# Earlier transfers in the even layer: load stage, attention projection, cached pages and sample outputs

## Chip, cores and metric

The kernel runs on one core of a Trainium2 chip. The metric is device time in microseconds for one execution. The engines of the core are TensorE (PE; its weight loads are shown as PEld), VectorE (DVE), ScalarE (ACT), GpSimd (POOL) and SyncE (SP). SP computes nothing here and issues nearly all transfers; its queue is shown as SPq.

## The reference

One inference step of a two-layer decoder trunk on a prompt of 1024 tokens and eight samples of four new tokens with a paged cache of 256 tokens each. Width 1024, all in float32. What matters here is the start of the first (even) layer:

```python
mod = silu(c) @ w_mod[l] + b_mod[l]
shift, scale, gate = split(mod, 3)
h = rms_norm(x, norm_w[l]) * (1 + scale) + shift
q_a, g_a, kv_a, z_a, z_b, xbc, dt_raw = split(h @ w_in_even)
q, k_cmp, k_slc, k_win = rope(...)              # rotary positions
past_kv = cache_nsa[page_table]                 # 8 samples x 2 pages of 128 tokens
kc, vc = compress(k_cmp), compress(v_cmp)       # silu((block + pe) @ w1) @ w2, blocks of 32 tokens
o = g0 * attend(q, kc, vc) + g1 * attend(q, ks, vs) + g2 * attend_window(q, kw, vw)
o_a = o * silu(z_a)
```

The prompt and the samples use the same weights. Later come a state-space mixer and the output projection of this layer, then a gated linear attention layer; the change doesn't touch them.

## The kernel before

The program is a sequence of blocks. In each one, every engine has its own list of instructions, the lists are tied by semaphores, and the block ends with a barrier of all engines. Work of one block therefore can't overlap that of the next, except for transfers that an earlier block issued and didn't wait for.

`block_load` (L212 to L363) brings in the rows of x, normalises them and transposes them into `hT`. It forms the modulation of layer 0 in two kinds, shift (i = 0) and scale (i = 1): `mod_products` on TensorE (64 matmuls for each half of 512 columns, banks 6 and 7), a copy on ScalarE, `mod_turn`, then `mod_finish` on VectorE. Last, ScalarE and VectorE apply scale and shift to `hT`. SP issues in this order: constants, c, x, four halves of w_mod of 2 MB each with one semaphore for each kind, the mask table, and the two attention weight tiles `w_attn[0]` and `w_attn[1]`, for which only the next block waits.

`block_attn_proj` (L379 on) projects to q (chunk 0), gates and the first part of kv (chunk 1) and the rest of kv (chunk 2), each in `NT` = 9 groups (one of samples, eight of 128 prompt rows). `w_attn` has two slots; slot 0 is loaded again for chunk 2. SP loads the rotation table and `pe_rows` at the head of the block, and TensorE's first instruction waits for both (`rope_in`). After chunk 2 SP writes the new kv rows out and waits for these writes at the end.

`block_past` (L609 on) reads the 16 cached pages into four slots of `page_rows`, each with one transfer from the page pool and one from the window cache. TensorE transposes each page, and behind every second page it does one of eight z products with the weights `w_za`. SP issues, after page 3, the eight transfers of `w_za`, and after page 5 the compression weights (four transfers of 0.5 MB) and `cmp_w2`. Page i waits until page i - 4 is transposed. Then TensorE runs the compression.

`block_attn_samples` (L741 on) attends for the samples. It writes its result to the scratch tensor `o_save` in memory, waits, reads it back as rows into `A.o_smp`, and waits again.

`block_attn_prompt` (L895 on) attends for the prompt in 72 units: for each of eight row tiles one compressed unit and eight others. For each unit TensorE does scores, transposes of the probabilities (`turn`) and values. The transposes are in groups, numbered in order; the number's parity gives the PSUM bank (4 or 5) and the engine that copies the group out (even: VectorE, odd: ScalarE). Group 0 was the turn of the sample outputs, ahead of all units. Behind the units 6, 14, 22 and so on stands a job of the late modulation.

## Time and profile before

| | us |
|---|---|
| median of three runs | 1896.12 |
| range of the runs | 1893.22 to 1897.64 |
| the profiled execution | 1895.02 |
| its span, first to last instruction | 1893.2 |

| stage (profiled execution) | begins at |
|---|---|
| block_load | 0 |
| block_attn_proj | 54.40 |
| block_past | 230.29 |
| block_attn_samples | 328.08 |
| block_attn_prompt | 378.42 |

TensorE is busy for 1667.0 us, 88% of the span; VectorE 39%, ScalarE 31%, GpSimd 20%. The mean granted clock of TensorE is 0.938 of full speed. The profile's page shows the whole; the views used below are the waits (who stood idle, and what released it), the timeline (instructions in order of time, with the idle time before them in brackets), the windows (busy time of each engine, granted clock and share of the DMA engines in a stretch) and the transfers with the time from issue to landing.

### The profile page before, as it was taken

The page shows a single profiled execution, that of the slowest core. Times are in us where ns is not written, and L with a number is a line of the kernel's source. Part 1 is how long each engine was busy: PE and PEld are TensorE (multiplying, and loading weights), DVE is VectorE, ACT ScalarE, POOL GpSimd, SP SyncE. Part 2 cuts the span into 40 slices and gives each one's busy share as a digit, 9 for nine tenths or more (in the row PEclk, how much of TensorE's full clock was granted, in tenths as well). Part 3 has the DMA queues.
Part 4 walks back from the last instruction along what each step waited for, and adds up shares of the span by engine and source line. Part 5 has one row for each costly group of instructions (what it writes and reads, how often), then busy time and mean ns, then how long its engine had stood idle before and what let it go on. Part 6 is the DMA issues. An engine that isn't in the chain of part 4 may idle for free. (4 is left out here: it accounts for less than half of the span.)

```text
span 1893.2 us, 27343 instructions
## 1 busy us (share of the span) xinstructions
PE 1667.0 (88%) x11621; PEld 1275.7 (67%) x11621; DVE 746.1 (39%) x1231; ACT 584.0 (31%) x1098; POOL 378.7 (20%) x234
## 2 busy tenths in 40 slices
PE   4799678699989879999999958898899989998698
PEld 4345447466666659999988736784899965554475
DVE  2211110145555546661078834223321444444443
ACT  4001110155544443222145533323330402222221
POOL 1111000011000012332179734110221230000231
PEclk8899889799999989999989978998899989998699
DMA  9120282142211001111101155112100130002521
GB/s 336 45 77 1 74 200 61 40 136 71 87 46 46 1 6 36 50 49 35 37 23 34 41 144 174 49 46 71 47 23 14 43 100 1 23 23 84 219 89 61
DMA packets 120573, 129.93 MB, mean 69 GB/s; under 512 B 16726, under 2 KB 92936, under 8 KB 120324
## 3 DMA queue, kind: packets, MB, share of 16 engines
q1 hardware_dynamic: 120100, 128.08, 21.6%
q8 instruction: 92, 1.51, 0.3%
q0 software_dynamic: 352, 0.10, 0.2%
q14 instruction: 29, 0.24, 0.0%
HBM read 107.05 MB, written 23.18 MB: 69 GB/s over the span
## 5 line engine op out<-in xcount | busy, mean ns | idle before, releaser
L154 PE MATMUL banks<-h_T_rest,w_ssd_high 128*128 128x352 f32 x480 | 156.0, 325 | 0.0
L154 PE MATMUL banks<-h_T_high,w_ssd_high 128*128 128x352 f32 x480 | 155.8, 325 | 0.0
L154 PE MATMUL banks<-h_T_high,w_ssd_rest 128*128 128x352 f32 x480 | 155.2, 323 | 0.0
L154 PE MATMUL banks<-w_attn,h_T 128*128 128x408 f32 (+5 forms) x432 | 147.8, 545 | 0.0
L154 PEld LDWEIGHTS banks<-w_attn,h_T 128*128 128x128 f32 (+1 forms) x432 | 73.9, 183 | 72.8 <-issue 55.6
L1165 DVE TENSOR_REDUCE neg_max_att<-banks 128x1 f32<-128x640 f32 (+7 forms) x128 | 88.8, 702 | 83.6 <-PE banks L154 83.3
L154 PE MATMUL banks<-w_r,h_T 128*128 128x512 f32 (+1 forms) x320 | 118.1, 556 | 0.0
L154 PE MATMUL banks<-out_even_w_high,mix_high 128*128 128x512 f32 (+1 forms) x216 | 87.9, 407 | 16.2 <-DVE out_even_w_rest L2070 12.3
L1104 ACT ACTIVATE p_att<-banks,neg_max_att 128x640 f32<-128x640 f32 (+7 forms) x128 | 89.6, 703 | 24.4 <-DVE neg_max_att L1165 23.7
L1042 PE MATMUL banks<-const_f,p_att 128*128 128x128 f32 x544 | 83.3, 285 | 15.1 <-DVE p_T_att L1170 8.3
L154 PEld LDWEIGHTS banks<-h_T_high,w_ssd_rest 128*128 128x128 f32 x480 | 90.9, 189 | 0.0
L154 PEld LDWEIGHTS banks<-h_T_high,w_ssd_high 128*128 128x128 f32 x480 | 90.2, 188 | 0.6 <-issue 0.6
L154 PEld LDWEIGHTS banks<-h_T_rest,w_ssd_high 128*128 128x128 f32 x480 | 90.1, 188 | 0.0
L1042 PEld LDWEIGHTS banks<-const_f,p_att 128*128 128x128 f32 x544 | 57.6, 141 | 47.7 <-issue 14.0
L154 PE MATMUL banks<-w_v_high,h_T_high 128*128 128x256 f32 (+1 forms) x288 | 82.9, 288 | 6.7 <-POOL w_v_rest L2398 6.7
L154 PEld LDWEIGHTS banks<-w_r,h_T 128*128 128x128 f32 (+1 forms) x320 | 50.2, 176 | 56.6 <-issue 55.1
L154 PE MATMUL banks<-out_even_w_rest,mix_high 128*128 128x512 f32 (+1 forms) x216 | 86.9, 402 | 0.0
L154 PE MATMUL banks<-out_even_w_high,mix_rest 128*128 128x512 f32 (+1 forms) x216 | 86.7, 401 | 0.0
L2751 DVE SCALAR_TENSOR_TENSOR gla_state<-gla_state,chunk_decay,banks 128x256 f32<-128x256 f32 x128 | 52.2, 475 | 86.4 <-PE banks L154 86.4
L1376 POOL TENSOR_TENSOR w_ssd_rest<-w_ssd,w_ssd_high 128x1024 fp32r<-128x1024 f32 x20 | 58.5, 2925 | 124.3 <-ACT w_ssd_high L1329 124.3
L154 PE MATMUL banks<-w_v_rest,h_T_high 128*128 128x256 f32 (+1 forms) x288 | 82.4, 286 | 0.0
L154 PE MATMUL banks<-w_v_high,h_T_rest 128*128 128x256 f32 (+1 forms) x288 | 81.7, 284 | 0.0
(475 smaller groups left out, 3496.6 us busy)
## 6 DMA issues: line engine op xcount, KB each, us to landing
w_mod_late<-in_w_mod_dram SPq DMA_DIRECT2D x8, 2048.0 KB
w_ssd<-in_w_in_even_dram SPq DMA_DIRECT2D x20, 512.0 KB, 3.8
w_mod_rows<-in_w_mod_dram SPq DMA_DIRECT2D x4, 2048.0 KB, 20.9
xin<-in_x_prompt_dram SPq DMA_DIRECT2D x8, 512.0 KB, 6.1
page_rows<-in_cache_nsa_dram SPq DMA_DIRECT2D x16, 256.0 KB, 2.7
cmp_w<-in_nsa_cmp_w_dram SPq DMA_DIRECT2D x8, 512.0 KB
silu_z_T<-in_state_ssd_dram SPq DMA_DIRECT2D x8, 512.0 KB, 4.3
out_dram<-silu_z_T SPq DMA_DIRECT2D x8, 512.0 KB, 3.5
```

The lines of the kernel that those rows point to most:

```text
L154: return nc.tensor.matmul(out, lhsT, rhs, start=start, stop=stop, skip_group_check=True)
L1042: last = nc.tensor.transpose(e.ps[:, 4 + g % 2, x * P:(x + 1) * P], src, e.ident)
L1104: nc.scalar.activation(p[:, n % 2, g, 0:counts[n] * P], head_scores(n, g), ACT.Exp, bias=neg[:, n % 4, g:g + 1], accum_out=den[:, i % 2, b ...
L1165: nc.vector.tensor_reduce(neg[:, n % 4, g:g + 1], head_scores(n, g), AX.X, ALU.max, negate=True).then_inc(neg_ready, 1)
L1376: nc.gpsimd.tensor_tensor(wlo[:, f % 2, :, :], w[:, f % 2, :, :], whi[:, f % 2, :, :].bitcast(F32), ALU.subtract).then_inc(w_rest, 1)
L2751: nc.vector.scalar_tensor_tensor(S[:, (n + 1) % NS, h, :], S[:, n % NS, h, :], Q.eb[:, h, n:n + 1], e.ps[:, j, x * LV:(x + 1) * LV], ALU.m ...
```

## The change

In the load stage each half of the modulation weights has a semaphore of its own, and TensorE waits for each half ahead of its products. The rotation table and the `pe_rows` are issued between the two attention weights. VectorE's copy of the masks moves behind the first `mod_finish`.

In the attention projection SP loads the page table and two pages at the head, and the `z_a` weights after chunk 1, into the place of slot 1 of `w_attn`. The pages lie where `o_smp`, `vcd` and `vcs` lie later, so GpSimd's memset of `vcd` now waits for the last page's transposes. `block_past` begins with page 2.

The sample outputs are read back by the first two transfers of the prompt attention, and they are turned and multiplied behind unit 8, as a group between those of the units. The groups of units 0 to 7 have numbers lower by one, so bank and copying engine are swapped for them; from unit 9 on they are as before.

```diff
@@ block_load
-        wmod_in = [new_sem(nc, f"w_mod_in{i}") for i in range(2)]
+        wmod_in = [[new_sem(nc, f"w_mod_in{i}{half}") for half in range(2)] for i in range(2)]
...
                 sp.dma_start(masks[:, :], e.k_masks).then_inc(masks_in, 16)
-                for i in range(2):
-                    load_attn_w(sp, e, e.w_attn[:, i], e.w_attn_in[i], ATTN_COLS[i])
+                load_attn_w(sp, e, e.w_attn[:, 0], e.w_attn_in[0], ATTN_COLS[0])
+                sp.dma_start(e.rope[:, :, :, :], e.k_rope.rearrange("p (a m d) -> p a m d", a=2, m=NT)).then_inc(e.rope_in, 16)
+                for j in range(2):
+                    sp.dma_start(e.pe_rows[:, j, :], e.nsa_cmp_pe[0].rearrange("v c d -> (v c) d")).then_inc(e.rope_in, 16)
+                load_attn_w(sp, e, e.w_attn[:, 1], e.w_attn_in[1], ATTN_COLS[1])
...
                 for i in range(2):
-                    pe.wait_ge(wmod_in[i], 32)
                     if i:
                         pe.wait_ge(mod_rows, i)
-                    mod_products(nc, e, wm[:, i, :, 0:512], 6)
-                    mod_products(nc, e, wm[:, i, :, 512:1024], 7).then_inc(mod_done, 1)
+                    for half in range(2):
+                        pe.wait_ge(wmod_in[i][half], 16)
+                        last = mod_products(nc, e, wm[:, i, :, half * 512:(half + 1) * 512], 6 + half)
+                    last.then_inc(mod_done, 1)
...
-                dve.wait_ge(masks_in, 16)
-                nc.vector.tensor_copy(e.kb[:, :], masks[:, :])
                 for i in range(2):
                     dve.wait_ge(mod_turned, i + 1)
                     mod_finish(nc, e, link, 0, i, 4, 0)
                     dve.sem_inc(mod_taken, 1)
+                    if i == 0:
+                        dve.wait_ge(masks_in, 16)
+                        nc.vector.tensor_copy(e.kb[:, :], masks[:, :])
@@ helpers
+PAGES_EARLY = 2
+
+def page_slot(A, i):
+
+    return A.pages[i % 4 // 2][:, i % 2, :]
+
+def load_page(sp, e, A, numbers, i):
+
+    number = sp.value_load(numbers[0:1, i:i + 1], min_val=0, max_val=NPOOL - 1)
+    src = e.cache_nsa[0][bass.ds(number, 1), :, :, :, :].rearrange("n t a g d -> (n t) (a g d)")
+    sp.dma_start(page_slot(A, i)[:, 0:512], src).then_inc(A.page_in[i % 4], 16)
+    sp.dma_start(page_slot(A, i)[:, 512:768], e.cache_nsa_win[0, i // NPG, (i % NPG) * PAGE:(i % NPG + 1) * PAGE].rearrange("t a g d -> t (a g d)")).then_inc(A.page_in[i % 4], 16)
@@ block_attn_proj
             def _(sp):
-                sp.dma_start(rope[:, :, :, :], e.k_rope.rearrange("p (a m d) -> p a m d", a=2, m=NT)).then_inc(rope_in, 16)
-                sp.dma_start(per[:, 0, :], e.nsa_cmp_pe[0].rearrange("v c d -> (v c) d")).then_inc(rope_in, 16)
-                sp.dma_start(per[:, 1, :], e.nsa_cmp_pe[0].rearrange("v c d -> (v c) d")).then_inc(rope_in, 16)
+                sp.dma_start(numbers[:, :], e.page_table.rearrange("b n -> (b n)").rearrange("(a n) -> a n", a=1)).then_inc(pt_in, 16)
+                sp.wait_ge(pt_in, 16)
+                for i in range(PAGES_EARLY):
+                    load_page(sp, e, A, numbers, i)
                 sp.wait_ge(proj_done, NT)
                 load_attn_w(sp, e, w[:, 0], w_in[0], cols[2])
...
+                sp.wait_ge(proj_done, 2 * NT)
+                wv = e.w_in_even[0, :, E_ZA:E_ZB].rearrange("(k p) n -> p k n", p=P)
+                for hh in range(HG):
+                    for g in range(G):
+                        sp.dma_start(A.w_za[:, :, hh * P + g * HD:hh * P + (g + 1) * HD], wv[:, :, (g * HG + hh) * HD:(g * HG + hh + 1) * HD]).then_inc(A.w_za_in, 16)
                 sp.wait_ge(rot_done, 3 * NT)
@@ block_past
-                for i in range(NP):
+                for i in range(PAGES_EARLY, NP):
                     if i >= 4:
                         sp.wait_ge(tr_done, i - 3)
...
-                    if i == 3:
-                        wv = e.w_in_even[0, :, E_ZA:E_ZB].rearrange("(k p) n -> p k n", p=P)
-                        for hh in range(HG):
-                            for g in range(G):
-                                sp.dma_start(A.w_za[:, :, hh * P + g * HD:hh * P + (g + 1) * HD], wv[:, :, (g * HG + hh) * HD:(g * HG + hh + 1) * HD]).then_inc(w_za_in, 16)
+                    load_page(sp, e, A, pt, i)
...
             def _(pool):
+                pool.wait_ge(tr_done, NP)
                 nc.gpsimd.memset(A.vcd[:, :, :], 0.0).then_inc(zeroed, 1)
@@ block_attn_samples
                 sp.wait_ge(o_out, 16 * DB)
-                for g in range(G):
-                    dst = A.o_smp[:, :].rearrange("p (h g d) -> p h g d", h=HG, g=G)[:, :, g, :]
-                    sp.dma_start(dst, e.o_save[:, g * HG * HD:(g + 1) * HG * HD].rearrange("t (h d) -> t h d", d=HD)).then_inc(o_out, 16)
-                sp.wait_ge(o_out, 16 * (DB + G))
@@ block_attn_prompt
+SAMPLES_AT = 8
...
-    engine_of.append(0)
-    order_of.append(1)
-    totals[0] = 1
...
+        if n == SAMPLES_AT:
+            sample_group = len(engine_of)
+            engine_of.append(0)
+            totals[0] += 1
+            order_of.append(totals[0])
...
             def _(sp):
+                for g in range(G):
+                    dst = A.o_smp[:, :].rearrange("p (h g d) -> p h g d", h=HG, g=G)[:, :, g, :]
+                    sp.dma_start(dst, e.o_save[:, g * HG * HD:(g + 1) * HG * HD].rearrange("t (h d) -> t h d", d=HD)).then_inc(o_smp_in, 16)
                 for f in range(2):
                     load_w_ssd(sp, e, S, f)
...
-                for hh in range(HG):
-                    last = nc.tensor.transpose(e.ps[:, 4, hh * TS:(hh + 1) * TS], A.o_smp[:, hh * P:(hh + 1) * P], e.ident[0:TS, 0:TS])
-                last.then_inc(t_done, 1)
+                def turn_samples():
+
+                    g = sample_group
+                    pe.wait_ge(o_smp_in, 16 * G)
+                    wait_copied(pe, g - 2)
+                    for hh in range(HG):
+                        last = nc.tensor.transpose(e.ps[:, 4 + g % 2, hh * TS:(hh + 1) * TS], A.o_smp[:, hh * P:(hh + 1) * P], e.ident[0:TS, 0:TS])
+                    last.then_inc(t_done, 1)
...
+                    if n == SAMPLES_AT:
+                        turn_samples()
...
-                dve.wait_ge(t_done, 1)
-                z = A.oT[:, :, TP:T]
-                nc.vector.tensor_tensor(z, e.ps[:, 4, 0:HG * TS].rearrange("p (h t) -> p h t", h=HG), z, ALU.mult).then_inc(copied_dve, 1)
...
+                    if n == SAMPLES_AT:
+                        dve.wait_ge(t_done, sample_group + 1)
+                        z = A.oT[:, :, TP:T]
+                        nc.vector.tensor_tensor(z, e.ps[:, 4 + sample_group % 2, 0:HG * TS].rearrange("p (h t) -> p h t", h=HG), z, ALU.mult).then_inc(copied_dve, 1)
```

## Rows read from the trace of the kernel before

**Rows 1.** The page's first line: the span of the profiled execution.

```profile
span 1893.2 us, 27343 instructions
```

**Rows 2.** Waits of TensorE, 0 to 380 us: waiter and releaser, total us, times, longest.

```profile
PE banks L667 <- DMA page_rows<-in_cache_nsa_win_dram: 13.6, 2, 12.8
PE banks L154 <- DMA w_z_a<-in_w_in_even_dram: 12.5, 1, 12.5
```

**Rows 3.** Timeline of TensorE, 35 to 60 us: start, duration, what, [idle before <- releaser].

```profile
35.48 3.70 PE L154 MATMUL banks<-w_mod_rows,modulation 128*32 128x128 f32 x128
...
41.96 5.37 PE L154 MATMUL banks<-w_mod_rows,modulation 128*32 128x128 f32 x128 [1.85 <-DMA w_mod_rows<-in_w_mod_dram]
47.82 0.44 PE L193 MATMUL banks<-const_f,mod_rows 128*128 128x128 f32 x2 [0.49 <-ACT mod_rows L327]
59.65 0.37 PE L473 MATMUL banks<-const_f,pe_rows 64*128 64x64 f32 x1 [11.39 <-DMA pe_rows<-in_nsa_cmp_pe_dram]
```

**Rows 4.** Timeline of VectorE in the load stage.

```profile
43.03 0.61 DVE L352 CAST const_bf<-mask_rows 128x864 bf16<-128x864 f32 x1 [7.40 <-DMA mask_rows<-in_k_masks_dram]
...
53.09 0.42 DVE L363 TENSOR_TENSOR h_T<-h_T,modulation 128x256 f32<-128x256 f32 x1
```

**Rows 5.** A window: length, busy PE, PEld, DVE, ACT, POOL, granted clock, DMA share, GB/s.

```profile
43.00:44.00 1.00, 1.00 (x28) 1.00 (x24) 0.75 (x2) 0.00 (x0) 0.00 (x0) 0.50 1.06 391
```

**Rows 6.** Timeline of SP's queue, load stage and head of the projection.

```profile
32.83 6.19 SPq L209 DMA_DIRECT2D w_attn<-in_w_in_even_dram  x2
54.40 0.34 SPq L417 DMA_DIRECT2D rope_table<-in_k_rope_dram  x1
```

**Rows 7.** The three transfers of line L209: time from issue to landing.

```profile
DMA to landing us min/median/max: 6.6/15.7/19.7
```

**Rows 8.** Timeline of TensorE: four transposes of 32 rows behind the second chunk.

```profile
172.03 0.40 PE L469 MATMUL banks<-const_f,q_rotated_samples 32*128 32x32 f32 x4 [0.29 <-ACT q_T L509]
```

**Rows 9.** Timeline of TensorE in the block of the past.

```profile
237.42 1.11 PE L667 MATMUL banks<-const_f,page_rows 128*128 128x128 f32 x4 [0.80 <-DMA page_rows<-in_cache_nsa_win_dram]
251.03 6.47 PE L154 MATMUL banks<-h_T,w_z_a 128*128 128x352 f32 x16 [12.50 <-DMA w_z_a<-in_w_in_even_dram]
...
258.21 4.90 PE L154 MATMUL banks<-h_T,w_z_a 128*128 128x352 f32 x16
...
296.69 10.91 PE L154 MATMUL banks<-cmp_in_T,cmp_w 64*128 64x96 f32 x128
```

**Rows 10.** Timeline of SP's queue in the block of the past.

```profile
230.29 0.23 SPq L634 DMA_DIRECT2D page_numbers<-in_page_table_dram  x1
...
234.07 0.35 SPq L641 DMA_DIRECT2D page_rows<-in_cache_nsa_dram  x1
...
238.58 8.54 SPq L648 DMA_DIRECT2D w_z_a<-in_w_in_even_dram  x8
...
250.41 5.18 SPq L632 DMA_DIRECT2D cmp_w<-in_nsa_cmp_w_dram  x4
255.62 2.24 SPq L652 DMA_DIRECT2D cmp_w<-in_nsa_cmp_w_dram  x1
```

**Rows 11.** Transfers from 228 to 268 us: count, KB each, us from issue to landing.

```profile
cmp_w<-in_nsa_cmp_w_dram SPq DMA_DIRECT2D x1, 64.0 KB, 7.5
```

**Rows 12.** Timeline of SP's queue, end of the samples and head of the prompt.

```profile
368.94 5.35 SPq L778 DMA_DIRECT2D o_save<-acc_samples  x8
375.41 0.83 SPq L782 DMA_DIRECT2D o_samples<-o_save  x2
378.42 1.03 SPq L1228 DMA_DIRECT2D w_ssd<-in_w_in_even_dram  x2
```

**Rows 13.** Timeline of TensorE in the prompt attention.

```profile
379.01 0.39 PE L154 MATMUL banks<-const_bf 128*128 128x128 bf16 x2
...
397.03 1.96 PE L154 MATMUL banks<-w_mod_late,modulation 128*32 128x128 f32 x64
```

**Rows 14.** A window in the prompt attention, columns as in rows 5.

```profile
388.00:400.00 12.00, 10.95 (x152) 7.32 (x152) 4.91 (x18) 6.62 (x26) 1.28 (x1) 1.00 0.08 29
```

More of the change, by code:

```diff
@@ L387, in block_attn_proj @@
         qrot8 = sb("q_rotated_samples", [P, 512])
-        rope = sb("rope_table", [P, 2, NT, HD])
+        rope, per, rope_in = e.rope, e.pe_rows, e.rope_in
+        numbers, pt_in = sb("page_numbers_first", [1, DB * NPG], I32), new_sem(nc, "page_table_first_in")
         t1, t2 = sb("rope_t1", [P, 2, 512]), sb("rope_t2", [P, 2, 512])
-        per = sb("pe_rows", [2 * CB, 2, HD])
-        rope_in = new_sem(nc, "rope_in")
         proj_done, q_freed, kv_freed = (new_sem(nc, s) for s in ("attn_proj_done", "q_bank_freed", "kv_bank_freed"))
@@ L614, in sb @@
             return ctx.enter_context(nc.sbuf_tensor(name, shape, dt))
-        page = sb("page_rows", [P, 4, 768])
+        A.pages.append(sb("page_rows", [P, 2, 768]))
         w1, w2 = sb("cmp_w1", [P, 2, CB // 2, 2 * HD]), sb("cmp_w2", [P, 2, HD])
@@ L666, in _ @@
                         at = j % 2 * P
-                        last = nc.tensor.transpose(e.ps[:, i % 2 + 2 * (j // 2), at:at + P], page[:, i % 4, s:s + P], e.ident)
+                        last = nc.tensor.transpose(e.ps[:, i % 2 + 2 * (j // 2), at:at + P], page_slot(A, i)[:, s:s + P], e.ident)
                     last.then_inc(tr_done, 1)
@@ L2110, in layer_even @@
     early = ExitStack()
+    A = Env()
+    with nc.sbuf_tensor("w_z_a", [P, KD, 512], F32, side="right") as A.w_za:
+        pass
+    A.w_za_in, A.page_in = nc.alloc_semaphore("w_z_a_in"), [nc.alloc_semaphore(f"page_in{i}") for i in range(4)]
     e.w_attn = early.enter_context(nc.sbuf_tensor("w_attn", [P, 2, KD, 512], F32, side="right"))
+    e.rope = early.enter_context(nc.sbuf_tensor("rope_table", [P, 2, NT, HD], F32, side="right"))
+    e.pe_rows = early.enter_context(nc.sbuf_tensor("pe_rows", [2 * CB, 2, HD], F32, side="right"))
+    e.rope_in = nc.alloc_semaphore("rope_in")
     block_load(nc, e, hT)
     with nc.sbuf_tensor("o_T", [P, 4, T], F32) as oT:
-        A = Env()
         A.hT, A.oT = hT, oT
@@ L2121, in layer_even @@
             A.peT, A.kccT = sb("pe_T", [P, 2 * CB]), sb("k_cmp_T", [P, NKEY // CB])
+            with nc.sbuf_tensor("page_rows_first", [P, PAGES_EARLY, 768], F32) as first:
+                A.pages = [first]
             A.o_smp = sb("o_samples", [TS, H * HD])
```

14 lines of the change are left out of this document (5 added, 9 removed).

## The prediction

> **What bounds the kernel now.** I read the span first [rows 1], then TensorE's waits over the first 380 us, then its instructions in order of time in each stage that the diff touches, and beside them SP's transfer queue. TensorE is the engine to follow: in these stages it is late only where it waits for a transfer. The list of waits has the two largest of them: 12.5 us for the z_a weights and 13.6 us for cached pages [rows 2]. Two more stand at the start: in the load stage TensorE idles 1.85 us before the second half of the modulation weights, and at the head of the attention projection it idles 11.39 us, released only by the small pe_rows transfer [rows 3]. A last one is at the start of the prompt attention, which cannot begin before SP has read the sample outputs back [rows 12]. Each of these is a stall in a serial chain of blocks, because every block ends with a barrier; time saved in one moves all that follows.
>
> **Part A, load stage and head of the projection.** Now the 128 modulation products of kind 1 wait for both halves of their weights, start at 41.96 and take 5.37 us; the 128 of kind 0 took 3.70 [rows 3]. The difference is the clock: from 43 to 44 us the granted clock was 0.50 (1.2 in place of 2.4 GHz) [rows 5], after the engine had been nearly idle from 39.18 (35.48 + 3.70) to 41.96 [rows 3]. The transfers arrive in the order of issue: the mask table is in by 43.03 [rows 4], the first attention weights 15.7 us after their issue at 32.83, at 48.5, and the second (issued at 33.4) 19.7 us later, at 53.1 [rows 6, 7]. So 2.1 MB take 5.5 us (43.0 to 48.5), and the first half of kind 1, one such piece ahead of 41.96, was in at about 36.5. With a semaphore for each half its 64 products run right behind the first turn, from about 40.1 to 41.95 (half of 3.70), and the second half from 41.96 to 43.8. That engine no longer idles for long, so I take the fast row: products end at 43.8 in place of 47.33, a gain of 3.5. With the slow row it would be 3.5 - 1.7 = 1.8. What follows (copy, turn, VectorE's passes over h_T) keeps its length, and VectorE ends at 53.51 - 3.5 = 50.0 in place of 53.51 [rows 4]. The next block's first transfer stands 0.89 us behind it, at 54.40 [rows 6]; so the next block could start at 50.9.
>
> The mask copy of 0.61 us is moved behind the first mod_finish. It would run at 43.03 to 43.64 as now, and the next turn of the modulation ends at about 44.7 (now 48.26, which is 0.93 behind 47.33), so it is hidden by 1 us; were it not, it would cost at most its 0.61.
>
> The rotation table (0.59 MB) and the two pe_rows now go between the two attention weights. Behind 48.5 they need 1.7 us at the 1.67 MB in 4.6 us (363 GB/s) of the second weights [rows 7], and small pieces and the last of 16 engines a little more: ready at about 51.0. TensorE then starts at 51.0 in place of 59.65 [rows 3]: **8.6 us gained**. The second attention weights come 1.7 us later, at about 55, for a chunk that is read only when the whole first chunk is through; free. The three issues leave SP's head of the projection (1.5 us) for the load stage, where SP is done at 39 [rows 6] and waits for nobody. The projection starts at the half clock as it does now; equal on both sides. The new page table load, its wait, and the four page transfers on SP stand at the head of the projection; behind them is only the reload of w_attn[0], which waits for the whole first chunk anyway. Free. The eight z_a weight transfers wait for the end of the second chunk, which is before the transposes at 172.03 [rows 8]; they take 8.54 us to issue and landed 12.45 us after the first issue [rows 9, 10], so they are in before 185, beside the third chunk, and SP is back at its wait for kv_rows before 181, while that chunk still runs. The tail of that block (writes of kv_rows, landing, barrier) is SP's and unchanged.
>
> **Part B, the past.** Now the block starts at 230.29 and its z products end at 296.69, that is 66.4 us, though the work is eight pairs of two page transposes and one z product. A pair takes 5.61 us: from 258.21 to 296.69 are seven z products and six pairs of pages, (296.69 - 258.21 - 4.90) / 6 [rows 9]. With pages 0 and 1 and the z_a weights in place nothing holds the first pair, so the work is 8 x 5.61 = 44.9. The start runs at the half clock after the idle tail of the block before: the first z product took 6.47 in place of 4.90 [rows 9], so 1.6 more. Pages 2 and 3 are issued where 0 and 1 are now and land by 237.42 [rows 9, 10]; the first pair ends at 230.3 + 5.6 + 1.6 = 237.5. Just in time. Pages 4 and 5 are issued from about 235.7 (1.5 us for each, as pages 1 to 3 between 234.07 and 238.58) and land by about 240.1, wanted at 243.1. Then comes what is **next in line**: the compression weights (four transfers of 0.52 MB, 5.18 us to issue) and w2, up to 2.24 us, which stand in SP's queue ahead of page 6 [rows 10]. Now the z_a weights are in at 251.03, and w2 lands 7.5 us after its issue, at 263.1 [rows 9 to 11]; between these lie pages 4 and 5, the compression weights and w2, 2.95 MB in 12.1 us, or 244 GB/s. In the new order 2.16 MB go from 240.1 to 249.0, page 6 lands at about 249.4 and page 7 at 251; they are wanted at 248.7 and 249.3. I take a new stall of 1.5 us, with 0 and 3.5 as ends. Later pages have 5.6 us for each pair, against 3 us of issuing. New length: 44.9 + 1.6 + 1.5 = 48.0, so **18.4 us gained** (16.4 to 19.9). The compression behind it keeps its length. The memset on GpSimd now waits for the last page's transposes; nothing is queued behind it, and its reader comes behind the whole compression.
>
> The Trainium skill, "DMA: Bandwidth & Descriptors", in its table of specifications, says that pieces below 512 bytes fall short of line rate; the z_a weights go in pieces of 256 bytes. The trace agrees in direction (2.1 MB in 12.45 us, against 5.5 for an equal load with longer pieces) [rows 9, 10], and by either rate they land beside the projection's third chunk, so the sum is the same.
>
> **Part C, sample outputs.** SP ends issuing o_save at 374.29, sees it landed at 375.4, issues two reads (0.83 us), waits for them, and the next block begins at 378.42 [rows 12]. Without the reads it begins 0.9 us behind 375.4 (the step from the last wait to the first instruction, as at 53.51 to 54.40): 376.3, a gain of 2.1. The four sample transposes leave the head: the first scores start at 379.01, 0.59 us behind the block's first transfer [rows 12, 13]; and they return behind unit 8, where four transposes of 32 rows take 0.40 at full clock [rows 8]. VectorE's product (0.3 us) runs beside. The reads are now ahead of w_ssd and the late modulation weights, 0.83 us; those are needed at 397.03 [rows 13], and DMA is at 0.08 from 388 to 400 [rows 14], so they had landed: hidden by 8 us. The new wait on TensorE (o_smp_in) stands behind 9 of 72 units, long after its two small transfers; behind it are queued unit 9 and all later ones, and none of them is held. VectorE's new wait is released by those transposes, and behind it stand its maxima for later units: at most the 0.40 us. The order of the copies of units 0 to 7 is swapped between ScalarE and VectorE, equal work in other hands; I bound that and the start at the half clock at 1 to 1.5 us either way. **2.2 us gained** (1 to 4).
>
> **Sum.** 8.6 + 18.4 + 2.2 = 29.2. The profiled execution took 1895.0 us (span 1893.2, [rows 1]); the median of the three runs is 1896.1. 1895.0 - 29.2 = 1865.8; on the median's scale 1866.9. I say 1866.
>
> **Rivals.** R1, the rotation table comes late. If transfers of the queue shared the engines rather than follow each other, table and second attention weights would end together, 1.7 us behind 53.1; TensorE would start at 54.8, and part A would be 4.9: 1869.6. Against it stand the three arrivals in order of issue. The Trainium skill, "DMA: Bandwidth & Descriptors", section on queues, rings and completion order, says that completion is not first-in first-out for an issuing engine. By that rule this rival is open; the trace speaks against it, since mask, first and second weights came in turn [rows 4, 7]. Chance 0.10.
>
> R2, the compression weights take the place of the z_a weights as the wait. If they went at the z_a weights' rate, 12.45 us for 2.1 MB, page 6 would land at about 252.9 and page 7 at 254.5, and the fourth pair would start 5.1 us late rather than 1.5: 1869.5; together with R1 1873. Chance 0.14.
>
> R3, slower than before. TensorE's clock falls to half in more of the prompt attention, because the swapped copies and the sample turn open small gaps; full clock is what it has there between 388 and 400 [rows 14]. Each us at half clock costs half a us. To lose the 29.2 and end 0.2% slower (3.8) it would take 66 us more at half clock, and the time would be 1900. Nothing in the rows leads there. Chance 0.02.
>
> R4, no change: the transfers would be late for another reason, as if SP's table load and its wait of 2 us held the first pair. TensorE's releasers are the very transfers that are moved [rows 2, 3], so I give it 0.02, at 1895.
>
> **How the numbers follow.** Forecast 0.72 at 1866, R1 0.10, R2 0.14, R3 0.02, R4 0.02. The low end takes no stall in B (1.5), part C at 4 (1.8), and the lowest run before (2.9 under the median): 1860. The high end takes R1 and R2 together with the slow row of part A: 1874.5. That is 1860 to 1875. About 0.2% (3.8 us) is what a measurement of this kernel can tell from no change. Faster 0.96, same 0.02, slower 0.02.
>
> **What would show it.** In the changed profile: the products of kind 1 in two runs without the idle 1.85 us, and the whole at full clock; TensorE's first matmul of the projection at about 51 with no wait for pe_rows; pages 0 and 1 and the first z product in one piece from the block's start, at about 221.7; a wait for page 6 or 7 of 0 to 3.5 us before the fourth pair; z products over 48 us after the block's start; SP's w_ssd issue about 1 us behind the block's start, which follows the o_save landing by 0.9. Wrong would be a longer wait for pages, a late rope_table or pe_rows, or a prompt attention longer than now by more than 1.5 us.

## The result, and the profile of the changed kernel

The changed kernel takes 1868.1 us (median of four runs, 1867.2 to 1870.0) where the kernel before takes 1896.9 (four runs, 1893.2 to 1898.8). The ratio is 0.9852, with a 95% interval of 0.9839 to 0.9865: 28.7 us less, against 1866.0 forecast and a range of 1860 to 1875. The profiled execution of the changed kernel took 1870.0 us.

The page's first line and its engines' busy times, to be read beside [rows 1]; ahead of them the second line of the page before:

```profile
PE 1667.0 (88%) x11621; PEld 1275.7 (67%) x11621; DVE 746.1 (39%) x1231; ACT 584.0 (31%) x1098; POOL 378.7 (20%) x234
```

```profile
span 1868.2 us, 27344 instructions
PE 1665.7 (89%) x11621; PEld 1275.3 (68%) x11621; DVE 744.2 (40%) x1232; ACT 583.4 (31%) x1097; POOL 379.4 (20%) x234
```

The span is 25.0 us shorter than in [rows 1]. VectorE has one instruction more (1232 for 1231) and ScalarE one less (1097 for 1098). The swapped group numbers do that: of the copies that take the transposed probabilities out of PSUM, VectorE has 78 in place of 77 and ScalarE 82 in place of 83. That one instruction will matter.

**Where the 25.0 us of the two profiles lie.** I took the start of each block from SP's and TensorE's timelines, in both traces, and subtracted:

| stretch | before | after | difference |
|---|---|---|---|
| span's start to the first matmul of the projection | 59.65 | 53.76 | -5.9 |
| projection, to the block of the past | 170.6 | 171.1 | +0.5 |
| past, to the end of its z products | 66.4 | 51.6 | -14.8 |
| compression | 31.4 | 30.8 | -0.6 |
| samples, to SP's first transfer of the prompt block | 50.3 | 48.3 | -2.1 |
| prompt attention, to the SSD projection | 317.3 | 317.7 | +0.4 |
| SSD projection, scan, all to the last block | 1075.7 | 1076.7 | +1.0 |
| last block (output of layer 2) | 121.8 | 118.3 | -3.5 |

Three lines are the three parts of the change. The last block is not one of them, and nobody edited it.

**Load stage.** TensorE's timeline (start, duration, what, idle before and its releaser), for [rows 3]:

```profile
37.59 3.70 PE L154 MATMUL banks<-w_mod_rows,modulation 128*32 128x128 f32 x128
...
42.15 0.42 PE L154 MATMUL banks<-w_mod_rows,modulation 128*32 128x128 f32 x6
43.02 3.65 PE L154 MATMUL banks<-w_mod_rows,modulation 128*32 128x128 f32 x122 [0.46 <-issue]
...
53.76 0.34 PE L499 MATMUL banks<-const_f,pe_rows 64*128 64x64 f32 x1 [6.18 <-PEq L141]
```

And the window that stood in [rows 5] at a granted clock of 0.50 (columns as there):

```profile
43.00:44.00 1.00, 0.98 (x36) 0.98 (x39) 0.00 (x0) 0.00 (x0) 0.00 (x0) 1.00 1.05 389
```

The second kind no longer waits for a transfer, only 0.46 us that the trace puts on nothing, and it runs at full clock. The first matmul of the projection is released by TensorE's own sequencer, that is by the start of the block, and no longer by pe_rows. SP's queue shows the tables where the diff put them, between the two attention weights:

```profile
34.47 5.46 SPq L246 DMA_DIRECT2D rope_table<-in_k_rope_dram  x1
39.98 1.97 SPq L248 DMA_DIRECT2D pe_rows<-in_nsa_cmp_pe_dram  x2
41.99 0.59 SPq L209 DMA_DIRECT2D w_attn<-in_w_in_even_dram  x1
```

**The past.** TensorE's timeline, for [rows 9]:

```profile
224.90 1.94 PE L684 MATMUL banks<-const_f,page_rows_first 128*128 128x128 f32 x8 [7.32 <-PEq L141]
226.63 6.16 PE L154 MATMUL banks<-h_T,w_z_a 128*128 128x352 f32 x16
...
246.82 2.04 PE L684 MATMUL banks<-const_f,page_rows 128*128 128x128 f32 x8 [2.81 <-DMA page_rows<-in_cache_nsa_win_dram]
248.66 5.40 PE L154 MATMUL banks<-h_T,w_z_a 128*128 128x352 f32 x16
253.89 1.04 PE L684 MATMUL banks<-const_f,page_rows_first 128*128 128x128 f32 x8
254.76 4.90 PE L154 MATMUL banks<-h_T,w_z_a 128*128 128x352 f32 x16
...
276.42 3.91 PE L154 MATMUL banks<-cmp_in_T,cmp_w 64*128 64x96 f32 x44
```

Both stalls of [rows 2] are gone. A new one stands before the fourth pair, for page 6, and behind it the next transposes and products are slow: 2.04 and 5.40 where the pair after it has 1.04 and 4.90. SP's queue says what stood ahead of page 6, for [rows 10], and the list of transfers of this stretch (count, KB each, us from issue to landing) when w2, the last of it, was in, for [rows 11]:

```profile
232.74 5.79 SPq L658 DMA_DIRECT2D cmp_w<-in_nsa_cmp_w_dram  x4
238.57 2.20 SPq L669 DMA_DIRECT2D cmp_w<-in_nsa_cmp_w_dram  x1
241.56 0.36 SPq L396 DMA_DIRECT2D page_rows<-in_cache_nsa_dram  x1
```

```profile
cmp_w<-in_nsa_cmp_w_dram SPq DMA_DIRECT2D x1, 64.0 KB, 7.3
```

w2 lands at 238.57 + 7.3 = 245.9, and page 6 right behind it: TensorE starts on it at 246.82.

**Samples and prompt.** SP's queue and TensorE, for [rows 12, 13]:

```profile
348.12 5.35 SPq L796 DMA_DIRECT2D o_save<-acc_samples  x8
355.49 0.83 SPq L1000 DMA_DIRECT2D o_samples<-o_save  x2
```

```profile
355.54 0.37 PE L154 MATMUL banks<-const_bf 128*128 128x128 bf16 x2 [12.90 <-PEq L141]
...
379.38 0.43 PE L1104 MATMUL banks<-const_f,o_samples 32*128 32x32 f32 x4
379.74 0.28 PE L154 MATMUL banks<-const_bf 128*128 128x128 bf16 x2
```

From the issue of o_save to the next block's first transfer it is 7.37 us, where it was 9.48. The moved sample transposes take 0.43 us and show no wait.

**The last block.** This is the stretch that the prediction never looked at. VectorE and GpSimd in the kernel before:

```profile
1803.02 3.32 DVE L2049 TENSOR_TENSOR mix_rest<-h_T,mix_high 128x1024 fp32r<-128x1024 f32 x1 [0.18 <-PE banks L154]
```

```profile
1802.92 2.34 POOL L2038 TENSOR_TENSOR out_odd_x_rows<-out_odd_x_rows,y_rows_out 128x1024 f32<-128x1024 f32 x1 [4.42 <-DVE y_rows_out L2087]
```

and in the changed one:

```profile
1781.67 1.21 DVE L2079 TENSOR_TENSOR mix_rest<-h_T,mix_high 128x1024 fp32r<-128x1024 f32 x1
```

```profile
1781.83 3.31 POOL L2068 TENSOR_TENSOR out_odd_x_rows<-out_odd_x_rows,y_rows_out 128x1024 f32<-128x1024 f32 x1 [4.47 <-DVE y_rows_out L2117]
```

The same two instructions meet in both. Whichever starts first takes its own time (GpSimd 2.34, VectorE 1.21), the other about the sum of both (3.32, 3.31). Before, GpSimd is first by 0.10 us and VectorE pays; after, VectorE is first by 0.16 us and GpSimd pays. Only VectorE's result is waited for, as TensorE's waits in the last block show (waiter and releaser, total, times, longest; before, then after):

```profile
PE banks L154 <- DVE mix_rest L2049: 3.6, 1, 3.6
```

```profile
PE banks L154 <- DVE mix_rest L2079: 1.2, 1, 1.2
```

and behind the longer wait the granted clock falls (windows of the eight us that follow; before, then after, columns as in [rows 5]):

```profile
1808.00:1816.00 8.00, 8.00 (x31) 6.50 (x31) 4.22 (x6) 1.35 (x3) 3.31 (x1) 0.84 0.38 131
```

```profile
1786.00:1794.00 8.00, 8.00 (x37) 6.60 (x37) 3.88 (x6) 2.62 (x6) 3.31 (x1) 1.00 0.41 131
```

2.4 us of wait (3.6 - 1.2) and about 8 x (1 - 0.84) = 1.3 us of clock make 3.7, near the 3.5 us of the table.

### The profile page after: what moved, and what is told of

The parts are those of the page before. It is cut to its first block and busy times, and to the rows that moved or that the text cites. A ratio compares the mean times of both kernels' runs of the same rounds, so it can differ in the third digit from the quotient of the medians.

```text
span 1868.2 us, 27344 instructions
## 1 busy us (share of the span) xinstructions
PE 1665.7 (89%) x11621; PEld 1275.3 (68%) x11621; DVE 744.2 (40%) x1232; ACT 583.4 (31%) x1097; POOL 379.4 (20%) x234
## 5 line engine op out<-in xcount | busy, mean ns | idle before, releaser
L154 PE MATMUL banks<-out_even_w_high,mix_high 128*128 128x512 f32 (+1 forms) x216 | 88.4, 409 | 16.7 <-DVE out_even_w_rest L2100 12.7
L1063 PE MATMUL banks<-const_f,p_att 128*128 128x128 f32 x544 | 83.3, 285 | 14.8 <-DVE p_T_att L1199 8.3
```

Of the source, the lines that this page charges most:

```text
L154: return nc.tensor.matmul(out, lhsT, rhs, start=start, stop=stop, skip_group_check=True)
L1063: last = nc.tensor.transpose(e.ps[:, 4 + g % 2, x * P:(x + 1) * P], src, e.ident)
```

## The experiments

The first four kernels were run against one set of runs of the kernel before (1897.6 us, 19 runs), the next four against another (1895.8, 7 runs), the last three against a third (1897.6, 15 runs). Each has its median, its ratio to its own kernel before, and the lengths of blocks in its profile. The lengths separate the parts more sharply than the times do: the same kernel's times spread over 2 to 11 us, while most blocks repeat to some tenths. Two don't: the block of the past with its new stall (50.4 to 51.6 us) and the scan (161.2 to 168.0).

**1. The load-stage part alone.** The hunks of block_load and the early rope_table and pe_rows; pages, z_a weights and sample outputs as before.

```diff
-PAGES_EARLY = 2
+PAGES_EARLY = 0
...
-                sp.wait_ge(proj_done, 2 * NT)
-                wv = e.w_in_even[0, :, E_ZA:E_ZB].rearrange("(k p) n -> p k n", p=P)
...
-SAMPLES_AT = 8
...
```

The lines show it against the changed kernel; block_attn_prompt and the end of block_attn_samples are those of the kernel before.

> Only the load stage's part of the change stands (halves, mask copy, rotation table and pe_rows); pages, z_a weights and sample outputs as before. Theory (gains of the blocks are serial and add): 8.6 us under the kernel before by the prediction, 5.9 if the later x rows of the changed kernel's profile (TensorE at the first modulation products 2.1 us later than before) are a cost of the change and not chance. Rival (the tables arrive with the second attention weights): 4.9. In the profile: first products of the modulation near 35.5 if it was chance, near 37.6 if it belongs to the change; first matmul of the projection at 51 or 53.7.

Measured: 1889.2 us (10 runs), ratio 0.9958 (0.9943 to 0.9972), so 8.3 us less (by the interval, 5 to 11). The projection starts at 53.39, the old block of the past takes 67.0, the last block 122.4. Part A is worth about what the sum said.

**2. Pages and z_a weights alone.** The semaphores of the load stage, the place of the tables and the sample outputs as before (the mask copy stays where the change put it); against the changed kernel:

```diff
-                    for half in range(2):
-                        pe.wait_ge(wmod_in[i][half], 16)
...
-                sp.dma_start(e.rope[:, :, :, :], e.k_rope.rearrange("p (a m d) -> p a m d", a=2, m=NT)).then_inc(e.rope_in, 16)
...
-SAMPLES_AT = 8
...
```

> Only pages 0 and 1 and the z_a weights are early; load stage and sample outputs as before. Theory: 66.4 us from the start of the past to the end of the z products become 51.6 as in the changed kernel, so 14.8 us under before (the prediction had 18.4), with a stall of about 2.8 us for page 6 and the clock at half behind it. Rival: the stall came from the shifted load stage, and without it the block takes 48, so 18.4.

Measured: 1878.0 us (4 runs), ratio 0.9896 (0.9870 to 0.9922), 19.5 us less. In its profile the block of the past takes 50.7 in place of 66.4, which is 15.7 and not 18.4; the stall for page 6 is there (3.2 us). But the slow products that were expected behind it are not:

```profile
256.02 0.66 PE L683 MATMUL banks<-const_f,page_rows 128*128 128x128 f32 x4 [3.22 <-DMA page_rows<-in_cache_nsa_win_dram]
```

```profile
257.45 4.90 PE L154 MATMUL banks<-h_T,w_z_a 128*128 128x352 f32 x16
```

The other 4 us of the time are not in the part: its scan block took 161.2 us against 166.1 before, which comes up below.

**3. The sample outputs alone**, here against the kernel before (the mask copy's place is also that of the changed kernel):

```diff
                 sp.wait_ge(o_out, 16 * DB)
...
-                sp.wait_ge(o_out, 16 * (DB + G))
...
+SAMPLES_AT = 8
...
+                    if n == SAMPLES_AT:
+                        dve.wait_ge(t_done, sample_group + 1)
```

> Only the reading back of the sample outputs is moved into the prompt attention. Theory: 2.1 us at the block's start and 0.1 to 0.2 from the turn, 2.2 under before, hard to tell from 0 with the spread of a time (0.2%); in the profile the step from the o_save issue (its end) to the next block's start falls from 4.1 to 2.0 us. Rival: the swap of the copies or the sample turn gives it back, 0 or above.

Measured: 1890.6 us (10 runs), ratio 0.9960 (0.9947 to 0.9972), 7.0 us less, which is three times what part C was forecast at. The profile gives 48.4 for the samples in place of 50.3, as expected; and 117.9 for the last block in place of 121.8. In experiments 1 and 2, which have the old prompt attention, that block keeps its 122.4 and 122.3. So the 4 us of the last block come with the edit of the prompt attention, 1400 us earlier. That was not understood yet; experiments 9 and 10 are for it.

**4. One semaphore for both halves.** The whole change, but with the old wait for 32.

```diff
-        wmod_in = [[new_sem(nc, f"w_mod_in{i}{half}") for half in range(2)] for i in range(2)]
+        wmod_in = [new_sem(nc, f"w_mod_in{i}") for i in range(2)]
...
+                    pe.wait_ge(wmod_in[i], 32)
                     if i:
                         pe.wait_ge(mod_rows, i)
```

> The changed kernel with one semaphore for both halves of each kind of modulation weights, as before. Theory: kind 1 waits for its second half and runs at the half clock again, 5.4 us in place of 3.7 to 4.1, so the changed kernel's time plus 1.8 to 3.5 us (1870 to 1871.6). Rival: the clock doesn't fall, plus 1.8 at the most. Or the apply stage is behind something else, such as the mask copy: plus 0.

Measured: 1871.8 us (4 runs), ratio 0.9874 (0.9845 to 0.9902). TensorE's timeline shows the wait back, and the slower products behind it:

```profile
43.02 5.03 PE L154 MATMUL banks<-w_mod_rows,modulation 128*32 128x128 f32 x128 [2.32 <-DMA w_mod_rows<-in_w_mod_dram]
```

From the start of the first products (36.07) to the projection (55.18) it is 19.1 us, where the seven kernels with halves and tables both have 16.1 to 16.7 (mean 16.4). The halves are worth 2.7 us.

**5. No early pages.**

```diff
-PAGES_EARLY = 2
+PAGES_EARLY = 0
```

> The changed kernel with no early page: block_past loads pages 0 and 1 itself, the z_a weights stay early. Theory: page 0 is in 5.2 us after the block's start and page 1 two us later, so the first pair starts at 5.2 and its second page at 7.1; with the page 6 stall (2.8 us) partly taken up in that, the time is 3 to 6 us above the changed kernel. Rival: pages are in order and every later one is late too, so the whole 7 us show.

Measured: 1869.3 us (4 runs), ratio 0.9856 (0.9829 to 0.9883). TensorE's timeline of the block's head, and the place where page 6 and 7 come:

```profile
228.02 1.11 PE L679 MATMUL banks<-const_f,page_rows_first 128*128 128x128 f32 x4 [12.35 <-DMA page_rows_first<-in_cache_nsa_win_dram]
230.28 1.11 PE L679 MATMUL banks<-const_f,page_rows_first 128*128 128x128 f32 x4 [1.15 <-DMA page_rows_first<-in_cache_nsa_win_dram]
...
249.19 0.66 PE L679 MATMUL banks<-const_f,page_rows 128*128 128x128 f32 x4 [0.17 <-DMA page_rows<-in_cache_nsa_win_dram]
```

The time is 1.1 us above the changed kernel's, where 3 to 6 were expected. The block takes 54.2 us, 2.6 more than in the changed kernel, though it starts its work 5.2 later and waits 1.15 once more. The stall before the fourth pair has shrunk to 0.17: a start that is late leaves the compression weights time to land. Of the 6.4 us that early pages save at the head, 2.6 remain; most of the rest is given back at page 6.

**6. z_a weights issued where they were, behind page 3.**

```diff
-                sp.wait_ge(proj_done, 2 * NT)
...
                     load_page(sp, e, A, pt, i)
+                    if i == 3:
+                        wv = e.w_in_even[0, :, E_ZA:E_ZB].rearrange("(k p) n -> p k n", p=P)
+                        for hh in range(HG):
...
```

> The changed kernel with the z_a weights issued behind page 3 in block_past, as before; pages 0 and 1 stay early. Theory: the first z product waits for the z_a weights, issued about 8 us behind the block's start where before it was 8.3, landing 12.5 later: so the pages alone bring nearly nothing (under 2 us) and the time is 13 to 15 us above the changed kernel. Rival: the early pages bring 5 us by themselves, and the time is 8 to 10 above.

Measured: 1874.6 us (4 runs), ratio 0.9878 (0.9851 to 0.9905). The wait of [rows 9] is back, and longer, since the pages no longer hold TensorE ahead of it:

```profile
240.59 7.17 PE L154 MATMUL banks<-h_T,w_z_a 128*128 128x352 f32 x16 [15.04 <-DMA w_z_a<-in_w_in_even_dram]
```

The block takes 63.4 us in place of 51.6: 11.8 of part B hang on these weights alone. The time is 6.5 us above the changed kernel's, under the 13 to 15 expected and under the rival's 8 to 10 too; its scan block took 161.2 us in place of 166.3, which makes up 5.1 us of the gap between 11.8 and 6.5.

**7. The compression weights out of page 6's way.**

```diff
-                    if i == 5:
+                    if i == 7:
                         load_w1(0)
+                    if i == 11:
                         load_w1(1)
...
```

> The changed kernel with the compression weights behind page 7 (first pair) and page 11 (second pair and w2) rather than all behind page 5. Theory (the weights ahead of page 6 in the queue are the new wait): no wait for page 6, no fall of the clock behind it, the fourth pair 5.9 in place of 7.4 and the stall of 2.8 gone: 4.3 us under the changed kernel, z products over in 47.5 us from the block's start. Rival (the page transfers themselves are short of rate, or the wait moves to pages 8 or 12): 0 to 2 under it.

Measured: 1862.1 us (4 runs), ratio 0.9808 (0.9780 to 0.9837), the best of its set. The first pair of the weights now stands behind page 7, the second pair and w2 behind page 11. SP issues page 6 at 232.37 and page 7 at 233.95, the first weights behind them, and the fourth pair has neither a wait nor the slow clock (SP's queue, then TensorE):

```profile
233.95 0.35 SPq L396 DMA_DIRECT2D page_rows<-in_cache_nsa_dram  x1
234.34 0.43 SPq L397 DMA_DIRECT2D page_rows<-in_cache_nsa_win_dram  x1
234.82 1.42 SPq L658 DMA_DIRECT2D cmp_w<-in_nsa_cmp_w_dram  x2
```

```profile
242.15 1.04 PE L685 MATMUL banks<-const_f,page_rows 128*128 128x128 f32 x8
243.03 4.90 PE L154 MATMUL banks<-h_T,w_z_a 128*128 128x352 f32 x16
```

The block takes 47.0 us: 44.9 for the eight pairs, as the prediction worked out, and 2.1 for the slow start. That settles the cause of the new stall, and its price in the changed kernel: 51.55 - 47.02 = 4.5 us. The time is 6.1 us under the changed kernel's, where 4.3 were expected; in the profiles the scan block, 164.5 us in place of 166.3, makes up the rest.

**8. The tables issued where they were.** rope_table and pe_rows at the head of the projection.

```diff
-                sp.dma_start(e.rope[:, :, :, :], e.k_rope.rearrange("p (a m d) -> p a m d", a=2, m=NT)).then_inc(e.rope_in, 16)
...
             def _(sp):
+                sp.dma_start(e.rope[:, :, :, :], e.k_rope.rearrange("p (a m d) -> p a m d", a=2, m=NT)).then_inc(e.rope_in, 16)
...
                 sp.dma_start(numbers[:, :], e.page_table.rearrange("b n -> (b n)").rearrange("(a n) -> a n", a=1)).then_inc(pt_in, 16)
```

> The changed kernel with the rotation table and pe_rows loaded at the head of the projection as before, ahead of the early pages. Theory: TensorE idles 5.2 us more at the head of the projection, so 5 us above the changed kernel, and the load stage is as in it. If the table in the load stage held anything else up, the difference is smaller.

Measured: 1873.5 us (4 runs), ratio 0.9867 (0.9838 to 0.9897). The old wait returns:

```profile
57.52 0.36 PE L499 MATMUL banks<-const_f,pe_rows 64*128 64x64 f32 x1 [11.61 <-DMA pe_rows<-in_nsa_cmp_pe_dram]
```

From the first products (35.76) it is 21.8 us against the mean of 16.4: the tables are worth 5.4 us.

**9 and 10. One VectorE instruction more.** VectorE's list is one instruction longer with the new prompt attention (1232 in place of 1231). To see whether that alone moves the last block, one idle memset of one element in each partition stands ahead of the loop over the units in block_attn_prompt, once in the kernel before (9), once in the changed one (10).

```diff
+                nc.vector.memset(neg[:, 3, 0:1], 0.0)
                 for n in range(-1, len(units)):
```

> The kernel before with one more VectorE instruction, a memset of one column ahead of the first unit of the prompt attention. Nothing else differs. It is for the last block (out_odd), which took 121.8 to 122.4 us in the three profiles of kernels with the old prompt attention and 117.9 to 118.6 in the seven with the new one. Theory S (VectorE's stream of instructions is one longer in the new one; in the last block mix_rest of row tile 2 then starts 0.26 us earlier, just ahead of a GpSimd operation rather than just behind it): the last block falls to about 118 and the whole time by about 4 us. Rival (a clock that happens to fall, or the place in time): last block 122, time as before.

Measured: 1893.7 us (10 runs), ratio 0.9979 (0.9969 to 0.9988): an added instruction that does nothing makes the kernel 3.9 us faster. Its last block takes 118.1 us, and VectorE is now ahead of GpSimd, as in the changed kernel:

```profile
1805.66 1.22 DVE L2050 TENSOR_TENSOR mix_rest<-h_T,mix_high 128x1024 fp32r<-128x1024 f32 x1
```

```profile
1805.82 3.30 POOL L2039 TENSOR_TENSOR out_odd_x_rows<-out_odd_x_rows,y_rows_out 128x1024 f32<-128x1024 f32 x1 [4.42 <-DVE y_rows_out L2088]
```

> The changed kernel with the same one memset more on VectorE. Theory S, if what counts is a narrow alignment of the stream: mix_rest starts behind GpSimd's operation again, last block 122, time 4 us above the changed kernel. If the stream only had to be one longer or more: 118 and no change. Rival: 118, no change, and no change in the kernel before either.

Measured: 1863.1 us (4 runs), ratio 0.9830 (0.9807 to 0.9854); the last block stays at 118.3. So a second instruction doesn't turn the order back. The stall for page 6 was there again, 2.93 and 0.36 us, and again without slow products behind it (4.90); its block of the past took 50.4 us. Of the thirteen profiled kernels the three with the old length of VectorE's list (before, 1, 2) have 121.8 to 122.4, and the ten with a longer one 117.8 to 118.6. That one instruction more moves mix_rest by the 0.3 us that decide is shown: in the kernel before it starts 1.40 us after the instruction ahead of it, in the changed one 1.14. Why it does is open. The row of the kernel before names TensorE as what released mix_rest, but TensorE's products and ScalarE's cast to mix_high stand at the same distances from that instruction in both kernels, to a few hundredths of a us, so they are not the difference.

**11. The two leads together.** Experiment 7, and the writes of kv_rows and gates with their wait moved from the end of the projection to the end of SP's list in block_past (12 transfers; the 20 of the expectation counts 8 that stay where they are). In the changed kernel TensorE stands still for 7.32 us ahead of the past, while SP issues these writes and waits for them.

```diff
-                sp.wait_ge(rot_done, 3 * NT)
-                sp.wait_ge(kv_freed, 2 * NT)
-                kv = A.kvrow
...
-                sp.wait_ge(rows_out, 16 * (2 * DB + 4))
...
                     load_w1(n)
+                rows_out = e.stored["kv_rows"]
+                kv = A.kvrow
...
+                sp.wait_ge(rows_out, 16 * (2 * DB + 4))
```

> The changed kernel with the compression weights spread behind pages 7 and 11, and with SP's writes of the kv rows and gates (20 small transfers, 9 us of issuing) and the wait for them moved from the end of the projection to the end of the block of the past. Theory: the projection then ends with TensorE's last transposes, and TensorE's idle 7.3 us there shrinks to about 1; with the 4.3 us of the compression weights, 10 to 11 us under the changed kernel, about 1857. SP has 12 us between its last load and the block's end, so the writes are hidden. Rival: the writes (9.3 us of issuing, 1.5 of landing) end behind TensorE in the block of the past and give part back: 4 to 8 under it.

Measured: 1852.3 us (5 runs), ratio 0.9774 (0.9759 to 0.9788), 45.3 us less than before, and 15.9 under the changed kernel's median; about 1857 was expected. TensorE at the head of the past:

```profile
216.82 1.06 PE L684 MATMUL banks<-const_f,page_rows_first 128*128 128x128 f32 x8 [1.02 <-PEq L141]
217.72 4.90 PE L154 MATMUL banks<-h_T,w_z_a 128*128 128x352 f32 x16
```

The idle time is 1.02 us in place of 7.32, and the first pair runs at full clock (1.06 and 4.90, against 1.94 and 6.16). The projection takes 164.1 us to the start of the past (171.1), the past 46.1 (51.6), and the compression keeps its 30.7: the writes are hidden in it. That is 12.5 us in the profiles; the rest of the distance to the changed kernel is mostly its scan block, 161.2 us in place of 166.3, in which nothing was edited.

## Why the prediction came out as it did, step by step

The total, 29.2 forecast and 28.7 measured, is closer than its terms, and that is luck: part B was too large by 2.4 to 3.6 us, and a gain that was not forecast, of 3.5 to 4, stood in for it. Without that gain the time would still lie inside the range, at about 1872.

**Part A, 8.6 forecast: right.** Alone it gave 8.3 us in time. In the profile the projection began at 53.76 rather than at 51.0, and two things are in that. The first products began at 37.59, against 35.48 before [rows 3]. Nothing in the change touches what comes ahead of them, and over the thirteen profiles this start lies between 34.5 and 37.6, with a mean of 36.2 for the seven with both halves and tables and of 36.2 for the four with neither: chance, with the kernel before at its early end and the changed one at its late end. Counted from that start, the projection begins 16.2 us on, where it was 24.2, so 8.0 gained against 8.6. The missing 0.6 is in kind 1: its products end 9.1 us after the start of kind 0, forecast 8.3, with the 0.46 us put on nothing the larger share of it. The kernel before was also a fast one of its kind: in the four profiles with the old load stage these 24.2 us are 24.2 to 26.1, mean 25.1, and kind 1 takes 5.0 to 6.5 us there. Against the mean of 16.4 that is 8.7 gained. The full clock was as forecast. Taken out of the whole change, the halves are worth 2.7 us (3.5 forecast) and the tables 5.4 (5.1 forecast). R1, a late table, did not happen: there is no wait for pe_rows or rope_table.

The prediction left this rival open by a sentence of the Trainium skill, "DMA: Bandwidth & Descriptors", on completion that isn't first-in first-out. The table sat between two weights of 2.1 MB and nobody waited for it, which agrees with the order of issue; no run here tells when exactly it landed.

**Part B, 18.4 forecast, 14.8 in the profile (15.7 alone): the mechanism right, two sizes off.** The eight pairs at 5.61 are exact: 44.9 + 2.1 = 47.0 is what experiment 7 measured. The step that failed is the new stall, 1.5 forecast. Two terms of it were mis-sized:
- The rate behind it. I took 244 GB/s for the 2.16 MB of compression weights, from the stretch in [rows 9 to 11]. In the changed kernel page 5 is issued at 232.3 and lands some 3 us later (an estimate: page transfers of this stretch take 2.8 to 3.3 us in the median), w2 is in at 245.9: 2.16 MB in 10.6 us, or 204 GB/s, between my value and R2's 168. The wait came to 2.81 us, between 1.5 and 5.1.
- The clock behind the wait. I priced the stall as idle time alone. The pair that follows took 2.04 + 5.40 in place of 1.04 + 4.90, another 1.5 us. Part A's own reading [rows 3, 5] had shown such products behind an idle time of 1.85 us; I used it there and forgot it here. This term does not always come: experiment 4 has it (2.67 us of wait, then 2.06 and 5.38), experiments 2 and 10 have waits of 3.22 and 2.93 us with products of 4.90 behind them, at a granted clock of 1.00. Why it falls in some executions and not in others is open.

The slow start was 2.2, not 1.6, since the page transposes at its head are slow too (1.94 for 1.04), and not only the z product. Together: 44.9 + 2.2 + 2.8 + 1.5 = 51.4, measured 51.6. So R2 named the mechanism that my forecast had at a third of its price: 4.3 of stall and clock, against 1.5 forecast and R2's 5.1. The bound of 0 to 3.5 was too narrow by the clock's share; in experiments 2 and 10, without that share, the two waits for pages 6 and 7 come to 3.5 and 3.3.

**Part C, 2.2 forecast: right, a little less.** The samples block gave 2.1, and w_ssd was issued 0.88 us behind the block's start (0.83 forecast). From the issue of o_save to the end of the prompt block it is 325.1 us after and 326.8 before, so 1.7 net: the first scores start earlier by 2.65 and the units then take 0.9 longer, inside the bound of 1 to 1.5 for the swapped copies. The new waits hold nobody; the late modulation products at 374.15 came without a wait.

**What no step held: the last block, 3.5 to 4 us.** Removing the head's product from VectorE's list and adding a wait and a product behind unit 8 was costed by what waits there, and that was right. But the prediction called the swapped copies "equal work in other hands", and they are not quite: one copy of 83 went from ScalarE to VectorE, whose list is one instruction longer for it. The order of two instructions on two engines turned 1400 us later. Experiment 9 shows that one more instruction on VectorE, with nothing else changed, is enough for this; that the swapped copy is what did it in the changed kernel is argued from there.

**The sum of the parts.** 8.3 (experiment 1), 15.7 (block of experiment 2), 1.7 and 3.5 to 4 make 29 to 30, against 28.7 measured; with the changed kernel's own 14.8 for the past it is 28 to 29. What is left is within the spread. A part of that spread has a place: the scan block took between 161.2 and 168.0 us in the thirteen profiles, with no edit in it. Its first 17 us in the kernel before and in experiment 2 (columns as in [rows 5]):

```profile
959.95:976.95 17.00, 15.19 (x69) 11.78 (x68) 11.88 (x12) 4.64 (x6) 7.92 (x5) 0.70 0.11 31
```

```profile
947.85:964.85 17.00, 15.19 (x105) 12.26 (x105) 16.36 (x16) 4.92 (x8) 12.41 (x7) 1.00 0.11 32
```

At a granted clock of 0.70 TensorE gets through 69 instructions there, at 1.00 through 105. The changed kernel's execution had 0.80 and 166.3 us, experiments 5, 6, 8 and 11 like experiment 2 161.2. It doesn't explain all: experiment 4 had 1.00 at the head and yet 164.6. This is where experiment 2's extra 4 us were. Whether the state at the head follows from when the block starts or from chance is open; no experiment was made for it.

**R3 and R4** did not occur: the prompt attention is 0.4 us longer, not 33, and the waits of [rows 2] went with their transfers.

## What to carry to other kernels

When a wait is removed, ask what is queued between the next data and its user, and price the new wait with two terms: its length, and the slow products that may follow. Here 2.8 us of wait cost 4.3 in one kernel, in two others waits of 3.3 and 3.5 us in all cost only themselves, and moving the transfers that stood ahead (two behind page 7, three behind page 11) took it all back. A block that ends with writes and a wait on them makes the tensor engine stand still and start the next one slowly; the writes can end in a later block with room. And a difference of 3 or 4 us in a stretch that nobody edited can be an order between two engines that hangs on a tenth of a microsecond: look there before it is credited to the edit.

## What was not expected of the hardware

**VectorE and GpSimd in each other's way.** The one that starts first takes what it needs, mix_rest 1.21 us or the addition to out_odd_x_rows 2.34; the one that starts second takes 3.3, with 0.10 us between the starts in one kernel and 0.16 in the other. The two don't share in proportion, or the first would be slowed too; the second waits: 2.34 - 0.10 + 1.21 = 3.45 against 3.32 measured, and 1.21 - 0.16 + 2.34 = 3.39 against 3.31. The Trainium skill, "SBUF — State Buffer", section "Who interferes with whom", says that a VectorE instruction with both inputs in SBUF contends with a GpSimd instruction that reads SBUF; its section "Terms" calls the shared pair of ports exclusive for a whole instruction, the loser blocking fully. Both instructions are of that kind here, and the trace agrees in the order and in the size.

**The projection at a slightly lower clock.** In the profiled execution of experiment 8 the granted clock stood at 0.95 for most of the projection, with TensorE busy throughout:

```profile
100.00:140.00 40.00, 40.00 (x112) 18.13 (x111) 8.12 (x21) 2.90 (x6) 7.83 (x7) 0.95 0.24 91
```

The same forty microseconds in the changed kernel have 1.00 and 120 instructions. The z products of the next block still take 5.11 us there in place of 4.90. The projection took 178.2 us in place of 171, and that execution, at 1878.1 us, is the slowest of its four (the others 1869.3 to 1874.5). A single profile would have put those 7 us on the tables.

**The start of the load stage.** The first modulation products begin between 34.5 and 37.6 us with the same instructions ahead of them. A gain of 2 us in this stage can't be read from one profile. Counted from the first products, the stage repeats to 0.6 us in the seven profiles with halves and tables, but only to 1.9 in the four with the old load stage.
